# Sample rows' attention on four column groups of TensorE, and an earlier load of FFN 2's first gate weights

## What is computed

```python
x = x + 0.5 * SwiGLU_1(rmsnorm(x))
p = rmsnorm(x) @ w_in            # A: q,k,v (8 heads x 64), B: q,k,v (8 heads x 64, rotary), indexer
# prompt: A is attention over a band of chunks, B over the 256 best keys that the indexer picks
# sample, for each stream b:
k = concat([k_cache[b], k_new[b]])              # 512 + 16 keys, 8 heads x 64
sc = einsum('qhd,khd->hqk', q, k) / 8 + bias    # A: relative bias; B: mask of the picked keys
o = einsum('hqk,khd->qhd', softmax(sc), v)      # v = concat([v_cache[b], v_new[b]])
x = x + concat(o_A, o_B) @ w_out
x = x + 0.5 * SwiGLU_2(rmsnorm(x));  y = rmsnorm(x)
```

## Time and profile before

| | us |
|---|---|
| median of 3 runs (2723.11 to 2723.99) | 2723.94 |
| the profiled execution, its own time | 2723.82 |
| its span in the trace | 2722.2 |
| PE busy | 2594.0 (95%) |
| sample items in the attention phase | 1594.2 to 1792.7 of the span |
| wo_phase | 1792.7 to 1918.8 |
| opening of FFN 2 | 1918.8 to about 1959 |

### The profile page before, as it was taken

The page is one execution under the profiler, slowest core; times in us unless marked ns, Lnnn a source line. Parts: engine busy times, 40 slices in busy tenths (PEclk is TensorE's granted clock), DMA queues, the critical chain, the costliest instruction groups (busy, mean ns, idle before and its releaser), DMA issues. The chain is left out here.

```text
span 2722.2 us, 40237 instructions
## 1 busy us (share of the span) xinstructions
PE 2594.0 (95%) x16684; PEld 2325.2 (85%) x16684; DVE 1324.4 (49%) x2297; ACT 986.6 (36%) x1671; POOL 510.4 (19%) x369
## 2 busy tenths in 40 slices
PE   6999999999998999988999999989799999999997
PEld 6999999988878799977887766658799999998886
DVE  6433332335553498977777723322732323333544
ACT  6433333234332323234666532221533333323432
POOL 0233333200001021750000000000134333310000
PEclk9999999999999999998999999989899999999999
DMA  3122212276632122214003315541122222245553
GB/s 124 49 82 65 82 65 82 72 272 221 217 128 67 51 93 73 67 51 144 25 32 102 124 64 188 171 172 47 55 82 65 82 65 82 65 151 213 210 201 124
DMA packets 153109, 294.27 MB, mean 108 GB/s; under 512 B 14033, under 2 KB 90457, under 8 KB 152929
## 3 DMA queue, kind: packets, MB, share of 16 engines
q1 hardware_dynamic: 146688, 268.12, 28.9%
q0 software_dynamic: 6240, 23.59, 2.4%
HBM read 237.26 MB, written 61.78 MB: 110 GB/s over the span
## 5 line engine op out<-in xcount | busy, mean ns | idle before, releaser
L803 DVE TENSOR_TENSOR f_dl<-f_raw_d,f_dh 128x2048 fp32r<-128x2048 f32 x66 | 151.3, 2293 | 271.4 <-ACT f_dh L619 271.4
L619 ACT ACTIVATE f_dh<-f_raw_d 128x2048 fp32r<-128x2048 f32 x66 | 126.5, 1916 | 319.0 <-PE f_pV L151 280.0
L569 ACT ACTIVATE f_gh<-f_pX 128x256 f32<-128x256 f32 x120 | 49.3, 411 | 318.8 <-PE f_pX L151 318.8
L1991 ACT ACTIVATE t_sc<-t_sc,t_small 128x640 f32<-128x640 f32 (+8 forms) x136 | 100.0, 735 | 143.3 <-DVE t_small L1920 110.4
L150 PE MATMUL f_pX<-f_xop,f_u_shi 128*128 128x256 f32 x504 | 149.2, 296 | 0.0
L151 PE MATMUL f_pX<-f_xop,f_u_slo 128*128 128x256 f32 x504 | 149.2, 296 | 0.0
L149 PE MATMUL f_pX<-f_xop,f_u_shi 128*128 128x256 f32 x504 | 149.2, 296 | 0.0
L149 PE MATMUL w_pw<-i_hi,r_T_hi 128*128 128x256 f32 (+1 forms) x504 | 145.7, 289 | 2.6 <-PEq L351 2.6
L150 PE MATMUL w_pw<-i_lo,r_T_hi 128*128 128x256 f32 (+1 forms) x504 | 145.0, 288 | 0.0
L151 PE MATMUL w_pw<-i_hi,r_T_lo 128*128 128x256 f32 (+1 forms) x504 | 144.4, 287 | 0.0
L150 PE MATMUL f_pX<-f_xop,f_g_shi 128*128 128x256 f32 x480 | 142.1, 296 | 0.0
(11 more groups left out here) (373 smaller groups left out, 8303.3 us busy)
## 6 DMA issues: line engine op xcount, KB each, us to landing
f_raw_d<-in_ffn_w_down SPq DMA_DIRECT2D x66, 1024.0 KB, 5.0
hid<-f_gh SPq DMA_DIRECT2D x22, 1152.0 KB, 8.8
f_raw_h<-hid SPq DMA_DIRECT2D x66, 384.0 KB, 5.6
f_g_raw<-in_ffn_w_gate SPq DMA_DIRECT2D x21, 1024.0 KB, 5.3
f_u_raw<-in_ffn_w_up SPq DMA_DIRECT2D x21, 1024.0 KB, 6.4
proj<-w_stage POOLq DMA_DIRECT2D x12, 1152.0 KB, 5.6
i_raw<-in_w_in SPq DMA_DIRECT2D x12, 1024.0 KB, 5.2
f_x<-in_x_prompt SPq DMA_DIRECT2D x16, 512.0 KB, 7.1
```

The costliest lines, as they stand in the source:

```text
L569: act.activation(dst, by_tile(pX[:, c, 0:N[c]]), ACT.Copy).then_inc(s_copy, 1)
L619: act.activation(d_hi[slot(q)][:], raw_d[slot(q)][:], ACT.Copy).then_inc(s_dhi, 1)
L803: dve.tensor_tensor(d_lo[slot(q)][:], raw_d[slot(q)][:], d_hi[slot(q)][:].bitcast(F32), ALU.subtract)
L1991: act.activation(sc_of(g, 0, n) if len(src.shape) == 2 else in_halves(sc_of(g, 0, n)), src, ACT.Exp, bias=small[:, 0, g % 4:g % 4 + 1], sc ...
```

## The change

Three things, and nothing else in the program.

1. **Four column groups.** `bd` shrinks to 128 x 32 for each head pair f, and `score` writes pair f to PSUM partitions 32f to 32f+31: four matmuls with 32 stationary columns, each its own accumulation group. In B items the mask product (bf16, 128 stationary columns) is still added over all 128 rows. `value` does the same: for each block of keys and each pair, 32 columns of exponentials by the pair's 128 value columns, to partitions 32f on. The result is 128 x 128 in place of 128 x 512; `osb` is scaled on 128 columns, and `out` is one transpose in place of four.
2. **FFN 2's first gate weights** are loaded by `FirstGate` within `wo_phase`, behind `w_out`, x and the norm's weights, into a place that is free in both phases (`wo_phase`'s norm buffers move to make it so). The load at FFN 2's start is gone.
3. **The opening's order** on ACT and DVE: the two halves of the weights' split stand ahead of the row tiles 0 and 1, and of 2 and 3; `row_sums` begin after tile 2's split.

SP's loop of the caches' loads is as it was.

```diff
@@ GateUpWeights
+        self.s_raw, self.s_hi, self.s_slo = ready.s_raw if ready else sem("loaded"), sem("hi"), sem("sums_lo")
+        self.zero = ready.raw if ready else self.raw
...
+    def act_open_hi(self, act, ks=(0, 4)):
         act.wait_ge(self.s_raw, 16)
-        for k in (0, 4):
-            act.activation(self.open_hi[:, k:k + 4, :], self.raw[:, k:k + 4, :], ACT.Copy).then_inc(self.s_ohi, 1)
+        for k in ks:
+            act.activation(self.open_hi[:, k:k + 4, :], self.zero[:, k:k + 4, :], ACT.Copy).then_inc(self.s_ohi, 1)
...
+HIDDEN_AT = SBUF_START + 736 + NT * 2 * NOP * 4 * HALF * 4
+class FirstGate:
+    def __init__(self, nc, ctx, w):
+        self.raw = nc.alloc_sbuf_tensor_at("first_gate", [P, KT, FB], F32, offset=HIDDEN_AT)
...
+    def load(self, sp):
+        sp.dma_start(self.raw[:], self.w_v[:, :, 0:FB]).then_inc(self.s_raw, 16)
@@ ffn_phase, sync
             else:
-                w[0].load(sp, 0)
                 w[1].load(sp, 0)
@@ ffn_phase, scalar
             else:
-                for t in range(4):
+                w[0].act_open_hi(act, (0,))
+                for t in range(2):
                     blocks_hi(t)
-                w[0].act_open_hi(act)
-                for t in range(4, NT):
+                w[0].act_open_hi(act, (4,))
+                for t in range(2, NT):
@@ ffn_phase, vector
             else:
-                for t in range(4):
+                w[0].dve_open_lo(dve, (0,))
+                for t in range(2):
                     blocks_lo(t)
-                row_sums(0)
-                w[0].dve_open_lo(dve)
-                row_sums(1)
+                w[0].dve_open_lo(dve, (4,))
+                for t in range(2, 4):
+                    blocks_lo(t)
+                    row_sums(t - 2)
@@ attn_phase
+PAIR = 2 * DEC_S
-        bd = [smp(f"bd{i}", [P, 5 * P], F32) for i in range(2)]
+        bd = [smp(f"bd{i}", [P, HT, PAIR], F32) for i in range(2)]
...
-                    dve.tensor_scalar(osb[:, n % 2, :], po[:], rec[:, n % 2, 0:1], None, ALU.mult).then_inc(s_os, 1)
+                    dve.tensor_scalar(osb[:, n % 2, 0:P], po[:, 0:P], rec[:, n % 2, 0:1], None, ALU.mult).then_inc(s_os, 1)
...
                         for f in range(HT):
-                            last = pe.matmul(out, bd[s % 2][:, f * P:(f + 1) * P], kTs[s % 2][:, f, c0:c1],
-                                             start=f == 0, stop=f == HT - 1 and x == 0)
+                            last = pe.matmul(out[f * PAIR:(f + 1) * PAIR], bd[s % 2][:, f, :], kTs[s % 2][:, f, c0:c1],
+                                             start=True, stop=x == 0)
...
-                    for k in range(PAST // P):
-                        pe.matmul(po[:], pT[:, s % 2, k * P:(k + 1) * P], vc[s % 2][:, k, :], start=k == 0, stop=False)
-                    pe.matmul(po[:], pT[0:DEC_S, s % 2, PAST:PAST + P], vn[s % 2][:], start=False, stop=True).then_inc(s_o, 1)
+                    for k in range(PAST // P + 1):
+                        for f in range(HT):
+                            cs, fs = slice(k * P + f * PAIR, k * P + (f + 1) * PAIR), slice(f * P, (f + 1) * P)
+                            new = k == PAST // P
+                            last = pe.matmul(po[f * PAIR:(f + 1) * PAIR, 0:P], pT[0:DEC_S if new else P, s % 2, cs],
+                                             vn[s % 2][:, fs] if new else vc[s % 2][:, k, fs], start=k == 0, stop=new)
+                    last.then_inc(s_o, 1)
                 else:
-                    pe_rows(pe, ("so", s), osb[:, (NTT + s) % 2, :])
+                    pe.transpose(pe_misc(pe, ("so", s))[:, 0:P], osb[:, (NTT + s) % 2, 0:P], ident[:]).then_inc(s_mf, 1)
@@ wo_phase, sync
             after.load(sp)
+            first_gate.load(sp)
```

More of the change, by code:

```diff
@@ L255, with __init__ @@
     BYTES = 8192 + 8192 + 4096 + 8192
-    def __init__(self, nc, new_sem, tag, at, w, base, ahead):
+    def __init__(self, nc, new_sem, tag, at, w, base, ahead, ready=None):
         place = lambda n, shape, dt, o: nc.alloc_sbuf_tensor_at(f"{tag}_{n}", shape, dt, offset=at + o)
@@ L275, in raw_of, with dve_open_lo @@
         return self.first if n == self.base else self.raw
-    def act_open_hi(self, act):
+    def act_open_hi(self, act, ks=(0, 4)):
         act.wait_ge(self.s_raw, 16)
-        for k in (0, 4):
-            act.activation(self.open_hi[:, k:k + 4, :], self.raw[:, k:k + 4, :], ACT.Copy).then_inc(self.s_ohi, 1)
-    def dve_open_lo(self, dve):
-        for k in (0, 4):
+        for k in ks:
+            act.activation(self.open_hi[:, k:k + 4, :], self.zero[:, k:k + 4, :], ACT.Copy).then_inc(self.s_ohi, 1)
+    def dve_open_lo(self, dve, ks=(0, 4)):
+        for k in ks:
             dve.wait_ge(self.s_ohi, k // 4 + 1)
-            dve.tensor_tensor(self.part[:, k:k + 4, :], self.raw[:, k:k + 4, :], self.open_hi[:, k:k + 4, :].bitcast(F32),
+            dve.tensor_tensor(self.part[:, k:k + 4, :], self.zero[:, k:k + 4, :], self.open_hi[:, k:k + 4, :].bitcast(F32),
                               ALU.subtract).then_inc(self.s_olo, 1)
@@ L337, in dve_sums_lo, with ffn_phase @@
         dve.tensor_tensor(self.slo[:, 2:4], self.sum[:, 2:4], self.shi[:, 2:4].bitcast(F32), ALU.subtract).then_inc(self.s_slo, 1)
-def ffn_phase(nc, tag, st, ident, x_rows, first, xhT, wg, wu, wd, g_next, hid, T, early, mid_of, store):
+HIDDEN_AT = SBUF_START + 736 + NT * 2 * NOP * 4 * HALF * 4
+class FirstGate:
+    def __init__(self, nc, ctx, w):
+        self.raw = nc.alloc_sbuf_tensor_at("first_gate", [P, KT, FB], F32, offset=HIDDEN_AT)
+        self.s_raw = ctx.enter_context(nc.semaphore("first_gate_loaded"))
+        self.w_v = w.rearrange("a (k p) f -> p (a k) f", p=P)
+    def load(self, sp):
+        sp.dma_start(self.raw[:], self.w_v[:, :, 0:FB]).then_inc(self.s_raw, 16)
+def ffn_phase(nc, tag, st, ident, x_rows, first, xhT, wg, wu, wd, g_next, hid, T, early, mid_of, store, ready=None):
     wd_v = wd.rearrange("a (n p) d -> p (a n) d", p=P)
@@ L354, in ffn_phase @@
         OPS = SBUF_START + 736
-        GH0 = OPS + NT * 2 * NOP * 4 * HALF * 4
+        GH0 = HIDDEN_AT
         UP = GH0 + 2 * ROWS * 4
@@ L361, in ffn_phase @@
         gh = [sb(f"gh{i}", [P, 2, ROWS], F32, at) for i, at in enumerate((GH0, GH1))]
-        w = [GateUpWeights(nc, sem, f"{tag}_g", GATE, wg, 1, GATE + 20480 if first else None),
+        w = [GateUpWeights(nc, sem, f"{tag}_g", GATE, wg, 1, GATE + 20480 if first else None, ready),
              GateUpWeights(nc, sem, f"{tag}_u", UP, wu, int(bool(first)), None if first else GATE + 20480)]
@@ L1856, in _ @@
                     pool.wait_ge(s_zero, 4)
-                bv = bd[s % 2][:].rearrange("p (f c) -> p f c", c=5 * DEC_S * 2)
+                bv = bd[s % 2]
                 for j, (dst, src) in enumerate(((kTs[s % 2][:, :, PAST:KS], snT[:, x, 0, :, bs]),
@@ L2207, in wo_phase @@
         raw = [keep(f"raw{i}", [P, D], F32) for i in range(2)]
-        norm = Plan(nc, tag, at_end(4 * D * 4))
-        assert keep.at <= norm.at
-        xn, g_bc = norm("xn", [P, 2, D], F32), norm("g", [P, D], F32)
-        junk = norm("junk", [P, D], BF16)
+        norm = Plan(nc, tag, at_selb)
+        xn, junk = norm("xn", [P, 2, D], F32), norm("junk", [P, D], BF16)
+        g_bc = keep("g", [P, D], F32)
+        assert keep.at <= HIDDEN_AT
         after = TileNorm(nc, ctx, tag + "b", st, ident, g_next, g_bc[:], junk[:], lambda t: x_sb[:, t, :], lambda t: xn[:, t % 2, :])
@@ L2357, in run_phases @@
                ((i["cache_a_k"], i["cache_a_v"]), (i["cache_b_k"], i["cache_b_v"])), *T, outs, head)
-    wo_phase(nc, at, x_sb, x_mid, two_rows, i["w_out"], T, xhT, st, ident, i["ffn2_norm"][0])
+    first_gate = FirstGate(nc, outer, i["ffn2_w_gate"])
+    wo_phase(nc, at, at_selb, first_gate, x_sb, x_mid, two_rows, i["w_out"], T, xhT, st, ident, i["ffn2_norm"][0])
     y_rows = rows_of(o["y_prompt"].rearrange("b s d -> (b s) d"), o["y_sample"].rearrange("b s d -> (b s) d"))
     ffn_phase(nc, "f2", st, ident, two_rows, None, xhT, i["ffn2_w_gate"], i["ffn2_w_up"], i["ffn2_w_down"],
-              i["final_norm"], hid, T, None, None, y_rows)
+              i["final_norm"], hid, T, None, None, y_rows, first_gate)
 _INS = ["x_prompt", "x_sample", "cache_a_k", "cache_a_v", "cache_b_k", "cache_b_v", "cache_idx_k",
```

5 lines of the change are left out of this document (2 added, 3 removed).

## The result

The changed kernel takes 2654.9 us, median of 4 runs (2653.24 to 2658.53), the kernel before beside it 2723.97 (4 runs): a ratio of 0.9747, interval 0.973 to 0.9764.

What follows compares the result with a forecast made beforehand. TensorE, busy 95% of the span, was taken to bound the kernel. From 2723.8 us, 50.7 off the sample items' stage and 3.6 off FFN 2's opening gave 2669.5; own range 2658 to 2696, wider range 2641 to 2700.

Steps and rivals of the forecast that it cites:

- the gap g: Per narrow matmul on TensorE, time to load the next weights: taken as 0.03 us, bounded by nothing and 0.09.
- rival 1: All four column groups run side by side, keys' loads bind all steps: stage -78, time 2642 us; chance 0.15.
- Side by side: Narrow passes on TensorE overlap only pairwise: score 2.06 us against 3.64, value 2.97 against 4.58.
- the second rival: The column groups don't overlap; the time is about 2720 us, the same within what can be told; chance 0.07.
- Out: TensorE's output transposes, three fewer per step: 0.33 us less, of which 0.15 was taken as gain.
- The wait that takes over: Keys' load, issued on SP after a value stage, binds A items at 8.43 us a step; B items, 8.98, don't wait.
- L: From the end of a value stage to the landing of the keys loaded after it: 0.96 + 7.5 = 8.46 us.
- A: TensorE's own step length without waiting for keys: 8.40 us in A items, 8.98 in B items.
- Rival 4: Granted clock falls through narrow matmuls and waits for keys in the sample items: about +55, 2780 us; chance 0.04.
- v0: First value stage's mark in the sample items, at 1622.54 before; forecast at 1616.2, by rival 1 at 1611.2.
- The mask products: Two 128-column products between narrow scores in each B item: 2 x 0.18 = 0.36 us for changing shape.
- FFN 2: Its opening: TensorE starts 4.1 us earlier, DVE's holes of 2.64 and 0.94 close, steady products come 3.6 earlier.

Runs made afterwards that it cites:

- One group at a time: Changed kernel with scores and cached values ordered so all passes of one column group follow each other: 2660.46 us, ratio 0.9765; with keys ahead added, 2650.78 us.
- keys ahead: Changed kernel with SP's load of keys s+1 moved ahead of the load of values s-1: 2631.51 us, ratio 0.9659.
- small loads: Changed kernel loading only one of four blocks of cached keys and values from item 2 on, TensorE's work the same, results not: 2629.19 us, ratio 0.965.
- the early load alone: Kernel before with FFN 2's first gate weights loaded in the output projection's phase, the opening's order as before: 2723.8 us, one execution.

## Why the prediction was right and wrong

- **Direction and size.** Faster by more than 0.2% (0.81), and in the range. Its own range, 2658 to 2696 by the gap g, misses the median. The wider range, 2641 to 2700, holds it because it was drawn to take in rival 1, not because the sum was right: the mechanism was rival 1's. That the median lies halfway between the two is luck in part: 6.5 us of low clock and some 5 us elsewhere in the stage, which rival 1's sum didn't have, moved it back towards a forecast with which they have nothing to do.
- **Side by side.** The step that failed is "a queue that starts matmuls in order, so I let the second pass of a pair overlap with the first of the next pair, not more". Score was forecast at 2.06, value at 2.97; measured are 0.91 and 1.00 + 0.35 (1619.08 to 1620.08, and 1614.29 to 1614.64 with the change back), the 0.9 and 1.4 of rival 1. (Groups that run concurrently are rival 1, not the second rival, as the prediction has it in one place.) One group at a time shows what is there in place of it: a group takes up to four passes while the next group's are started, and within that the groups don't wait for one another.
- **The gap g** for the load of the next weights does not appear: four score passes take 0.91, as four of 0.228 do, and the passes of a group start 0.109 apart throughout the value stage, from one matmul to the next too. The 0.12 that the value stage has over its eight passes stands once, ahead of the new values.
- **Out.** The -0.15 did not come: from the output's transposes to the scores it is 1.16 us with keys ahead, 1.15 before (1660.04 to 1661.19 in the earlier trace rows), with three transposes less. The scores stand 0.26 and 0.27 behind the end of the copy of the last keys in both traces, so this copy is what they wait for, and the 0.26 that the rows seemed to leave was none.
- **The wait that takes over.** L = 8.46 was right: 0.96 from issue to issue and 7.5 to the landing stand in the rows after. So was the rule (L + A) / 2, as a mean of a short and a long step. It was applied to the wrong A: with 5.8 in place of 8.40 it gives 7.1 in A items, as rival 1 has it, and in B items with 6.5 it binds too (7.5), where the forecast had no wait.
- **The clock.** Rival 4 named it with narrow matmuls or waits as cause. The narrow matmuls are none, as keys ahead shows with 1.00. The waits are: six of 1.9 to 3.1 us, and 21 us at the lower level. From v0 to v13 it is 102.6 us; the same work at full clock without waits takes 81.2 with keys ahead, the waits are 14.9, and the 6.5 left over go with the clock. The 1.4 a step that rival 4 had from rival 1 was a mean: in fact every second step has a wait of up to twice that. That the clock falls with such waits and stays up without them is what the changed kernel's trace and those of keys ahead and of small loads show; how long a wait must be is open (one group at a time has waits of 0.7 to 1.6 us and a mean clock of 0.96).
- **From rival 1 to the measured stage** (-78 against -66.0): v0 came 1.3 later than its sum (the 2.3 by which the stage began later taken off), v0 to v13 took 102.6 where it had 93.3, 6.5 of it by the clock, and from v13 to the end of the stage 11.6 where it had 10.2.
- **The mask products.** Priced at 0.18 for the change and 0.11 of their own, each; measured (1.60 - 0.91) / 2 = 0.345, of which 0.24 is the change. The price of the change was too small by a quarter, at 8 items a matter of 1 us.
- **FFN 2.** Mechanism and order right: the first product at 4.77 (4.7 said), the product on `f_u_slo` 3.8 earlier in its phase (3.6 said), and DVE's holes of 2.64 and 0.94 gone. The 3.8 is at the upper end: between the other kernels with the old and with the new order it is 1.6 to 3.2, and the phase as a whole is 2.8 shorter. So 3.6 was somewhat high. "The load's new place costs nothing" holds by the early load alone. That both edits are needed, the prediction didn't say.

## What to carry to other kernels

When a change halves an engine's step, work out first which transfer then comes last, and from which instruction its issue hangs: here 23 us more, a third of what the change itself gave, lay in the order of two loads in SP's loop, which did nothing as long as TensorE was slow. A wait hides the cost of other edits beside it (1.4 us a step showed as 5.6 us in all with the wait, as 19.3 without), so judge an edit again once the wait is gone. Matmuls on few columns are worth spreading over the column groups so that neighbours in the program differ in group.

## What the runs showed of the hardware

- Float32 matmuls of 32 columns on four column groups run fully side by side: 16 passes of 264 columns in 0.91 us, 32 passes of 128 in 1.00.
- The groups are not served in program order: with eight passes of one group in a row the 32 passes take 2.36 us, not 3.2, and each group starts with the fifth pass of the one ahead; with four in a row nothing is lost.
- A change from 32 columns to 128 and back costs about 0.24 us.
- With waits of 1.9 to 3.1 us in every second step the granted clock was 0.57 to 0.76 in the stretches quoted; the same matmuls without waits kept 1.00. The low clock behind the waits cost 6.5 us on top of their 14.9.
- With the DMA engines busy at 0.94 (324 GB/s) the keys' loads took 7.9 us at the median, 7.5 in the kernel before at about half that share. The two are not quite alike: the 7.5 is of a load issued 0.96 us behind another of 1 MB.
